# Attention outputs in three stages produced transposed, with a pair's values as stationary operand and both heads' weights as 256 moving columns

## The reference

```python
def _memory_attention(qm, mem, mem_norm, w_mem_kv):
    kv = _rmsnorm(mem, mem_norm) @ w_mem_kv
    s = jnp.einsum('bshd,bmhd->bhsm', qm, mk) * (HEAD_DIM ** -0.5)
    p = jax.nn.softmax(s, axis=-1)
    o = jnp.einsum('bhsm,bmhd->bshd', p, mv)
...
    # layer B, own block
    p = jax.nn.softmax(jnp.where(kpos <= qpos, s_own, NEG), axis=-1)
    o = jnp.einsum('bhqk,bkhd->bqhd', p_own, v_own)
    x = x + jnp.concatenate([o_self, o_mem], axis=-1) @ b_w_out[j]
...
    # layer C
    logits = jnp.where(valid[:, None], logits + bias, -jnp.inf)
    p = jax.nn.softmax(logits, axis=-1)
    out_a = jnp.einsum('bhtk,btkd->bthd', p, vg)
    x = x + jnp.concatenate([out_a, out_b], axis=-1) @ w_out[l]
```

## Time and profile before

| what | value |
|---|---|
| median of 3 runs | 915.58 us (914.89 to 916.04) |
| profiled execution, first to last instruction | 915.4 us |
| PE busy | 907.2 us, 99% of the span |
| PE weight loads | 767.8 us, 84% |
| DVE, ACT, POOL busy | 593.7, 490.4, 61.3 us |
| granted TensorE clock, mean of the span | 0.996 of full speed |
| chain that ended last | PE 96%, DVE 2%, ACT 1% |

### The profile page before, as it was taken

The page is one execution under the profiler, slowest core; times in us unless marked ns, Lnnn a source line. Parts: engine busy times, 40 slices in busy tenths (PEclk is TensorE's granted clock), DMA queues, the critical chain, the costliest instruction groups (busy, mean ns, idle before and its releaser), DMA issues.

```text
span 915.4 us, 13523 instructions
## 1 busy us (share of the span) xinstructions
PE 907.2 (99%) x4824; PEld 767.8 (84%) x4824; DVE 593.7 (65%) x898; ACT 490.4 (54%) x750; POOL 61.3 (7%) x124
## 2 busy tenths in 40 slices
PE   9999999999999999999999999999999999999998
PEld 7778788888888888888888888888788888888887
DVE  4768858555555686746855555667987466555565
ACT  6756666444444566754644444465577464444452
POOL 1102122000000000000200000013130000000000
PEclk9999999999999999999999999999998999999999
DMA  8945137665555453424966555545441447556551
GB/s 297 335 139 183 49 138 236 212 196 183 183 188 193 168 176 103 134 97 149 328 204 197 199 186 184 148 137 197 170 161 43 142 139 230 184 183 188 190 172 47
DMA packets 96885, 159.88 MB, mean 175 GB/s; under 512 B 5969, under 2 KB 37921, under 8 KB 96841
## 3 DMA queue, kind: packets, MB, share of 16 engines
q1 hardware_dynamic: 94240, 155.08, 51.1%
q10 hardware_dynamic: 2568, 4.21, 1.3%
q0 software_dynamic: 32, 0.02, 0.0%
HBM read 158.21 MB, written 3.16 MB: 176 GB/s over the span
## 4 chain that ended last, share of the span: by engine, by line
PE 96%; DVE 2%; ACT 1%; issue 0%; POOL 0%; ACTq 0%; POOLq 0%; DVEq 0%
PE turn L1660 10%; PE proj L1660 9%; PE proj L1604 6%; PE proj L1606 6%; PE proj L1605 6%; PE score L1604 6%; PE score L1605 6%; PE score L1606 6%; PE outp L1604 5%; PE outp L1606 5%; PE outp L1605 5%; PE turn L1664 5%; PE proj L1664 5%; PE outp L1839 3%; PE score L1802 2%; PE turn L1650 2%
## 5 line engine op out<-in xcount | busy, mean ns | idle before, releaser
L1931 DVE TENSOR_TENSOR wlo<-raw,whi 128x2048 fp32r<-128x2048 f32 (+1 forms) x131 | 297.3, 2278 | 171.8 <-ACT whi L1350 132.7
L1350 ACT ACTIVATE whi<-raw 128x2048 fp32r<-128x2048 f32 x64 | 122.7, 1917 | 162.5 <-PE turn L1664 76.2
L1339 ACT ACTIVATE whi<-raw 128x2048 fp32r<-128x2048 f32 (+1 forms) x67 | 126.3, 1896 | 63.3 <-PE proj L1606 16.9
L1604 PE MATMUL proj<-whi,set 128*128 128x512 f32 (+1 forms) x270 | 106.6, 395 | 0.0
L1606 PE MATMUL proj<-whi,set 128*128 128x512 f32 (+1 forms) x270 | 103.8, 384 | 0.0
L1605 PE MATMUL proj<-wlo,set 128*128 128x512 f32 (+1 forms) x270 | 103.5, 383 | 0.0
L1660 PE MATMUL turn<-set,whi 128*128 128x512 f32 x384 | 96.3, 393 | 0.0
L1660 PE MATMUL proj<-set,whi 128*128 128x512 f32 x384 | 95.6, 391 | 0.0
L1604 PE MATMUL score<-whi,set 128*128 128x512 f32 x236 | 93.0, 394 | 0.0
L1605 PE MATMUL score<-wlo,set 128*128 128x512 f32 x236 | 92.1, 390 | 0.0
L1606 PE MATMUL score<-whi,set 128*128 128x512 f32 x236 | 92.0, 390 | 0.0
(11 more groups left out here) (231 smaller groups left out, 1318.5 us busy)
## 6 DMA issues: line engine op xcount, KB each, us to landing
raw<-in_a_w_up SPq DMA_DIRECT2D x32, 512.0 KB, 4.3
raw<-in_a_w_down SPq DMA_DIRECT2D x32, 512.0 KB, 4.5
raw<-in_b_w_up SPq DMA_DIRECT2D x32, 512.0 KB, 4.4
raw<-in_b_w_down SPq DMA_DIRECT2D x32, 512.0 KB, 4.5
raw<-in_w_gate SPq DMA_DIRECT2D x22, 512.0 KB, 4.0
raw<-in_w_up SPq DMA_DIRECT2D x22, 512.0 KB, 5.0
raw<-in_w_down SPq DMA_DIRECT2D x22, 512.0 KB, 4.1
raw<-in_a_w_in SPq DMA_DIRECT2D x20, 512.0 KB, 6.7
```

What stands on the lines that cost most here:

```text
L1339: return act.activation(shaped(whi, u)[:, ks, :], shaped(raw, u)[:, ks, :], ACT.Copy)
L1350: act.activation(shaped(whi, u), shaped(raw, u), ACT.Copy).then_inc(hi_done, 1)
L1604: pe.matmul(out_, hi, wh, start=start, stop=False)
L1931: return dve.tensor_tensor(shaped(wlo, u)[:, ks, :], shaped(raw, u)[:, ks, :], shaped(whi, u)[:, ks, :], ALU.subtract)
```

## The change

For memory, causal and selected items (the differential ones stay as they are):

- `mix` multiplies `e` in place by the reciprocals, both heads in one DVE instruction of 2n columns, and `turn_weights` waits for it (`w_done`).
- `attend` takes the values of the pair, 128x128, as the standing operand and lets the transposed weights of both heads move, 256 columns, once per block of keys. The output is [values of two heads, head, query], and of its four quadrants of 64x128 two are wanted.
- The evacuation writes operands directly: ACT copies the two quadrants to the high part (`o_hi`), DVE subtracts for the low part (`o_evac`). For layer A's memory items these lie in a new buffer, `mem_out`; `operand()` finds them.
- `turn_operand` of outputs goes: half of the second bank pair in layer A, both in layer B, that of the selected heads in layer C. What a wait for it was is now a wait for `o_evac`.
- The key/value tile `qk` has 20 blocks instead of 24, one bias table and the late gains move to other buffers, and the value shared by selected heads is copied twice, side by side.
- The tables of `MOVES` for PE, DVE and ACT are new and longer, and POOL gets one.

```diff
--- before.py
+++ after.py
...
-        ("multiply 74", "turn_operand 34"), ("turn_weights 38", "attend 36"), ("turn_weights 37", "attend 35"),
...
+        ("turn_weights 39", "multiply 74"), ("turn_weights 38", "turn_weights 39"),
...
+    "POOL": [
+        ("split 6", "diff_norm 0"), ("multiply 6", "split 6"), ("statistics 1", "multiply 6"),
...
+        mem_out = sb("mem_out", [P, 2, 2, TOK], F32R)
...
-        def turn_operand(src, half, gains, ready, set_free, cols=None):
-
-            use = [t_use(), t_use()]
-            for b in range(2):
+        def operand(lhs, part, k):
+
+            if lhs == MEM_OUT:
+                return mem_out[:, k - 6, part, :] if k >= 6 else sets[1][:, k, part, :]
+            return sets[lhs][:, k, part, :]
+
+        def turn_operand(src, half, gains, ready, set_free, banks=2):
+
+            use = [t_use() for _ in range(banks)]
+            for b in range(banks):
                 st = add("turn_operand")
                 st.src, st.half, st.gains, st.ready, st.set_free = src, half, gains, ready, set_free
                 st.b, st.use, st.hi = b, use, count.hi
-            count.hi += 2
+            count.hi += banks
...
-        def attend(it, vneed):
+        def attend(it, vneed, lhs=1):
             it.o, it.o_free = o_use()
             it.vneed = vneed
             if it.kind == "diff":
                 count.osq += 1
                 it.osq = count.osq
+            else:
+                count.out += 1
+                k = it.pair + (6 if it.kind == "mem" else 0)
+                it.out, it.turned = count.out, [operand(lhs, part, k)[:, tok(it.t)] for part in range(2)]
             st = add("attend")
...
-        def finish_attention(w, items, o_half, last_qset_unit, oset, gain, vneed, around):
+        def finish_attention(w, items, o_half, last_qset_unit, gain, vneed, around):
 
             ua, ub, uc, ud = out_units(w)
-            o1 = turn_operand(o_nat, 0, [(None, oset, 0)], (o_evac, o_half), 2 * last_qset_unit + 2)[-1]
+            diff = items[0].kind == "diff"
+            o1, lhs = (o_evac, o_half), 1
+            if diff:
+                o1, lhs = turn_operand(o_nat, 0, [(None, 1, 0)], o1, 2 * last_qset_unit + 2)[-1], MEM_OUT
             attend(items[0], vneed); attend(items[1], vneed)
             turn_weights(items[2]); turn_weights(items[3])
-            if items[0].kind == "diff":
+            if diff:
                 norm(items[0:2])
 
             def last_items():
                 done = around()
                 attend(items[2], vneed)
                 o_all = attend(items[3], vneed)
-                if items[0].kind == "diff":
+                if diff:
                     norm(items[2:4])
                 return o_all, done
 
-            o_all, done = multiply_around(last_items, ua, oset, 0, o1, "P", True, False)
+            def last_turned():
+                if not diff:
+                    return o_evac, o_all
+                return turn_operand(o_nat, 1, [(None, 1, UK)], (o_evac, o_all), 0, banks=1)[-1]
+
+            o_all, done = multiply_around(last_items, ua, lhs, 0, o1, "P", True, False)
             split(ua + AHEAD)
-            o2 = multiply_around(lambda: turn_operand(o_nat, 1, [(None, oset, UK)], (o_evac, o_all), 0)[-1],
-                                 ub, oset, 0, o1, "S", True, False)
-            return out_tail(ub, (uc, oset, UK, o2), (ud, oset, UK, o2), 1 - oset, gain), done
+            o2 = multiply_around(last_turned, ub, lhs, 0, o1, "S", True, False)
+            return out_tail(ub, (uc, lhs, UK, o2), (ud, lhs, UK, o2), 0, gain), done
...
-        o1 = turn_operand(o_nat, 0, [(None, 1, 0)], (o_evac, o_a), 0)[-1]
+        o1 = (o_evac, o_a)
...
-                    elif it.kind == "idx":
+                    else:
                         act.wait_ge(o_full, it.o + 1)
-                        act.wait_ge(w_done, it.w)
                         for c in range(2):
-                            at = it.pair * P + c * DH
-                            ins = act.activation(o_nat[:, it.t, at:at + DH], Ob[it.o % 2][:, c * DH:(c + 1) * DH],
-                                                 ACT.Copy, scale=it.rs[:, c:c + 1])
-                        ins.then_inc(o_evac, 1)
+                            ins = act.activation(it.turned[0][HALF[c]], Ob[it.o % 2][HALF[c], tok(c)], ACT.Copy)
+                        ins.then_inc(o_hi, 1)
...
-                        ins = act.activation(v[:, t, 512:512 + DH], Sb[s % 2][:, t * P + DH:t * P + P], ACT.Copy)
+                        value = Sb[s % 2][:, t * P + DH:t * P + P].unsqueeze(1).broadcast_to([P, 2, DH])
+                        ins = act.activation(v[:, t, 512:512 + P].rearrange("p (c n) -> p c n", c=2), value, ACT.Copy)
...
-                    if it.kind == "diff":
-                        pe.wait_ge(w_done, it.w)
-                    else:
-                        pe.wait_ge(exp_done, it.exp + 1)
+                    pe.wait_ge(w_done, it.w)
...
-                    for c in range(1 if it.kind == "diff" else 2):
-                        for k in range(nk):
-                            b = c * nk + k
-                            wt = wT[:, it.buf, b * P:(b + 1) * P]
-                            h = 2 * it.pair + c
-                            dst = O[:, c * DH:(c + 1) * DH]
-                            if it.kind == "diff":
-                                val, dst = v[:, k, it.pair * P:(it.pair + 1) * P], O[:, 0:P]
-                            elif it.kind == "mem":
-                                val = memkv[:, 1, k * 256 + h * DH:k * 256 + (h + 1) * DH]
-                            elif it.kind == "causal":
-                                val = v[:, k, h * DH:(h + 1) * DH]
-                            else:
-                                val = v[:, k, 512:512 + DH]
-                            ins = pe.matmul(dst, wt, val, start=k == 0, stop=k == nk - 1)
+                    cols = slice(it.pair * P, (it.pair + 1) * P)
+                    for k in range(nk):
+                        if it.kind == "diff":
+                            wt = wT[:, it.buf, tok(k)]
+                            ins = pe.matmul(O[:, 0:P], wt, v[:, k, cols], start=k == 0, stop=k == nk - 1)
+                            continue
+                        if it.kind == "mem":
+                            val = memkv[:, 1, k * 256 + it.pair * P:k * 256 + (it.pair + 1) * P]
+                        elif it.kind == "causal":
+                            val = v[:, k, cols]
+                        else:
+                            val = v[:, k, 512:512 + P]
+                        wt = wT[:, it.buf, 0:2 * it.n].rearrange("p (c n) -> p c n", c=2)[:, :, tok(k)]
+                        ins = pe.matmul(O[:, 0:TOK].rearrange("p (c n) -> p c n", c=2), val, wt, start=k == 0,
+                                        stop=k == nk - 1)
                     ins.then_inc(o_full, 1)
...
                 elif st.kind == "mix":
                     it = st.it
                     dve.wait_ge(exp_done, it.exp + 1)
-                    ins = dve.reciprocal(it.rs, it.rs)
+                    behind(dve.reciprocal(it.rs, it.rs))
                     if it.kind == "diff":
-                        behind(ins)
                         behind(dve.tensor_tensor(it.rs[:, 1:2], it.rs[:, 1:2], lam[:, 4:5], ALU.mult))
                         e0, e1 = e[:, it.buf, 0:it.n], e[:, it.buf, it.n:2 * it.n]
                         behind(dve.tensor_scalar(e1, e1, it.rs[:, 1:2], None, ALU.mult))
                         ins = dve.scalar_tensor_tensor(out=e0, in0=e0, scalar=it.rs[:, 0:1], in1=e1,
                                                        op0=ALU.mult, op1=ALU.subtract)
+                    else:
+                        both = heads_view(e[:, it.buf, 0:2 * it.n], 2)
+                        ins = dve.tensor_tensor(both, both, spread(it.rs, it.n), ALU.mult)
                     ins.then_inc(w_done, 1)
                 elif st.kind == "attend":
                     it = st.it
-                    O = Ob[it.o % 2][:, 0:P]
-                    at = it.pair * P + (SELF if it.kind == "mem" else 0)
-                    dst = o_nat[:, it.t, at:at + P]
-                    if it.kind not in ("diff", "idx"):
-                        dve.wait_ge(o_full, it.o + 1)
-                        dve.wait_ge(w_done, it.w)
-                        dve.tensor_tensor(heads_view(dst, 2), heads_view(O, 2), spread(it.rs, DH), ALU.mult)\
-                           .then_inc(o_evac, 1)
+                    if it.kind != "diff":
+                        dve.wait_ge(o_hi, it.out)
+                        for c in range(2):
+                            ins = dve.tensor_tensor(it.turned[1][HALF[c]], Ob[it.o % 2][HALF[c], tok(c)],
+                                                    it.turned[0][HALF[c]], ALU.subtract)
+                        ins.then_inc(o_evac, 1)
...
```

(8 more changed lines are left out.)

28 lines of the change are left out of this document (16 added, 12 removed), and 183 rows, old and new, of the table MOVES.

## The result

| | before | after |
|---|---|---|
| median of the runs beside each other (5 each) | 915.58 us (914.89 to 917.16) | 921.83 us (920.85 to 922.03) |
| profiled execution, first to last instruction | 915.4 us | 919.4 us |
| that execution's own time | not listed | 921.14 us |

The change made the kernel slower: ratio 1.0061, 95% interval 1.0050 to 1.0072. I had forecast 914.9 and a range up to 918.6.

What follows compares the result with a forecast made beforehand. PE, busy 99% of the span, was taken as the bound, with its waits. Terms +0.7 - 3.05 - 0.6 - 0.2 + 1.6 + 0.9 = -0.65 us on the profiled 915.4, 0.2 under the median, gave 914.9; range 911.0 to 918.6.

Steps and rivals of the forecast that it cites:

- (a): Attend on PE's row: 92 instructions of 256 columns at 0.225 us replace 184 of 64 columns, +0.7 us (0 to +1.5).
- (b): Transposes of outputs on PE: 28 of 64 go and all of it counts, -3.05 us (-3.1 to -2.9).
- (c): Start: eight transposes of the memory input fill PE's wait for the first weights, -0.6 us, or 0.
- (d): Layer A's last output: the 0.9 us wait for the operand's DVE half comes behind two attends, -0.2 us (-0.9 to 0).
- (f): Start of stage C's selected heads: select rounds and multiplies stand ahead of steps PE needs, +0.9 us (0 to +1.5).
- the memory stages' waits, put at 0: Memory stages: weight products hide reciprocal and multiply (0.6 to 0.85 us), so 0; if the cover goes, +2 us.
- (e): End of the causal heads, where nothing covers: ACT's 10.1 us beside PE's 9.1 adds waiting, +1.6 us (-0.8 to +3).
- The recorded walk: End of the causal heads, stepped through from the end of the value products: 2.0 to 2.8 us late, 0.8 there before.
- stage C keeps its clock: Rival, stage C: its waits fall apart into short ones and 3.4 us of lost clock comes back, 911.5 us; chance 0.10.
- The waits are covered: Rival, causal heads' end and stage C's selected start: the added waiting there is 0, 912.4 us; chance 0.22.
- The causal stretch loses the clock: Rival, causal stretch: PE's pauses add up to 2 to 3 us and the clock falls, 918.3 us; chance 0.16.
- DVE sets the pace in the memory stages: Rival, memory stages: DVE gets 0.6 to 0.85 us more per item, +2 us, 916.9 us; chance 0.08.

Runs made afterwards that it cites:

- second profile: Kernel before, unchanged, timed and profiled again: 915.49 us median, the profiled execution with a span of 913.8 us.
- e10: Before, with 12 filling identity transposes in stage C's wait and the memory input's second half turned ahead of the first weight products: 914.76 us.
- e5: After, with the low part of one weight block moved behind the norm of items d8, d9 on DVE in layer A: 920.58 us.
- e2: After, without the multiply of e by the reciprocals; turn_weights of memory, causal and selected items waits for the exponentials alone: 918.17 us.
- e6: After, with ACT's copy of c5's turned weights moved ahead of the exponentials of c6 and c7: 922.96 us.
- e11: After, with ACT's output copies of 28 items doubled, the extra ones to a spare tile nobody reads: 929.32 us.
- e12: After, without the multiply of e, with layer A's low part behind the norm and stage C's wait filled with identity transposes: 915.47 us.
- e3: After, with three places of its order changed, on DVE (layer A, causal stretch, stage C) and ACT (copies of turned weights): 927.33 us.

## Why the prediction was wrong

**The miss.** The time is 6.9 us above the forecast. 1.5 of it is the last step of the sum, from the span to the time: I took 0.2 for it, and it is 1.7 (921.14 for a span of 919.4 after, 915.52 for 913.8 before). Another 0.7 is after's median above its profiled execution. The other 4.7 are the three attention parts, which against the first profile missed by 3.0 (A), 1.2 (B) and 0.5 us (C).

**What held.** (a) and (b), by after's groups:

```profile
L1922 PE MATMUL outp<-wT,v 128*128 128x256 f32 x60 | 16.0, 388 | 0.7 <-ACT wT L1574 0.5
...
L1922 PE MATMUL outp<-wT,memkv 128*128 128x256 f32 x32 | 8.1, 382 | 0.5 <-issue 0.5
...
L1737 PE MATMUL turn<-ident,o_nat 128*128 128x128 f32 x36 | 5.8, 304 | 0.2
```

92 instructions of 256 columns; two take 0.43 us from start to start at 392.84 below, 0.215 each against the 0.225 that I took, so 92 cost 19.8 us for 20.0 before: -0.2 where the term had +0.7. 36 transposes are left of 64. (c) The start saved: 0.4 to 0.7 as measured by e10, for 0.6. (d) The wait of 0.9 became 0.8, but the term had its place wrong: in before it stands at 114.78 and 115.38, ahead of transposes of e, and not at the last output, whose transposes at 125.04 waited for nothing. (f) Behind the gain op, DVE's timeline reads

```profile
687.84 1.66 DVE L2383 TENSOR_TENSOR o_nat<-o_nat,zq 128x512 f32<-128x512 f32 x1
689.53 0.43 DVE L2354 MAX8 stat<-wT 128x8 f32<-128x256 f32 x1
...
690.51 0.29 DVE L2239 CUSTOM_DVE_ANT_0 e<-score,memkv 128x128 f32<-128x128 f32 x1
```

with 2.67 us from the gain op to the maxima at 690.51. In before the gain op starts at 684.27 and the maxima at 685.96, 1.69 later. That is the round of 0.98 that the term names. Turn_weights starts 5.3 us behind the gain op (693.16) instead of 3.8 (688.11), for a forecast of 1.2 more.

**What failed first: the memory stages' waits, put at 0.** The step read "I put it at 0; if the cover goes, eight items would show up to 0.25 each". Attention A missed by 2.6 us. e5 accounts for 1.25 of it, a collision of DVE and GpSimd that no term had, and e2 for 0.8, the multiply. That 0.8 is the memory stage: in e2 the wait of 0.49 ahead of the memory attend at 92.69 is gone, and this attend starts at 92.03. So the cover went at one place, and the multiply's price was put at 0 for it. The other 0.5 is not isolated.

**Second, the size of (e).** The mechanism was right and the size was not. PE's timeline of after from attend c2 to attend c8:

```profile
392.84 0.59 PE L1922 MATMUL outp<-wT,v 128*128 128x256 f32 x2
...
399.04 0.63 PE L1899 MATMUL turn<-ident,e 128*128 128x128 f32 x4 [0.88 <-ACT wT L1574]
...
402.89 1.10 PE L1922 MATMUL outp<-wT,v 128*128 128x256 f32 x4 [0.49 <-ACT wT L1574]
...
405.04 0.70 PE L1922 MATMUL outp<-wT,v 128*128 128x256 f32 x2
405.54 0.51 PE L1691 MATMUL proj<-whi,set 128*128 128x512 f32 x1
```

12.7 us for 9.1 of work, 3.6 of waiting; before had 0.8. So the term was +2.8, forecast at +1.6 and bounded by +3. The chain there names who held PE:

```profile
397.14 0.68 ACT e L1583 x3
...
398.00 0.27 ACT set L1595
...
398.29 0.61 ACT wT L1574
...
399.04 0.64 PE turn L1899 x4
...
402.19 0.61 ACT wT L1574
...
402.89 1.12 PE outp L1922 x4
```

It is ACT's row of exponentials, output copies and weight copies, as worked out (10.1 us beside 9.1). The recorded walk has no wait for c5's weights. It puts ACT's exponentials of c6 and c7 at 2.2 to 3.9 us from the end of the value products, and they ran at 3.1 to 4.9, since DVE took the maxima of c6 only behind four subtractions:

```profile
394.17 1.21 DVE L2262 TENSOR_TENSOR set<-outp,set 64x128 fp32r<-64x128 f32 x4
395.41 0.29 DVE L2239 CUSTOM_DVE_ANT_0 e<-score,cmask 128x128 f32<-128x128 f32 x1
```

The copy of c5's weights stood behind them, at 398.29. e6 shows that taking it ahead does not help, e11 that more of the same costs half its length, and e12 that 2.2 of the 2.8 stay when the multiply is gone.

**Third, what stood at (f) besides the term.** Attention C missed by 2.5 against the second profile. e2 gives 1.5 of it to the multiply, where I had 0.3. The clock gives 0.5 net: PE's wait there grew to 2.18 us,

```profile
691.71 0.38 PE L1885 MATMUL score<-selmask,identb 128*128 128x128 bf16 x4 [2.18 <-DVE stat L2239]
```

and the low clock came behind it in each profile of the change with that wait left open. Here my reading of before was wrong at the base. I took the earlier trace rows for what before does and "stage C keeps its clock" for a rival in which the change gains 3.4. Before keeps its clock throughout in 24 of 70 executions, and of after's five none does, so the fall is a loss that comes and goes before and is nearly regular with the change (e2 has one execution of eleven at full clock, e11 one of four). The +0.2 between span and median hid this; the offset is 1.7.

**The rivals.** "The waits are covered" fell by e2, e5 and e11. "The causal stretch loses the clock" did not occur in after (its windows there read 1.00) but did in e3 once waits of 0.8 and 1.5 stood together. "DVE sets the pace in the memory stages" was nearest to attention A, by another mechanism. No single rival reached 921.8; the range had them one at a time, and what happened was more waiting in all three attention parts at once.

**The ledger,** on 915.4, before's time at full clock: about -3.7 on PE's row (-3.05 transposes, -0.2 attend from start to start, -0.4 the start), +3.7 multiply (3.0 by the spans), +1.25 collision, +1.0 clock with its waits (0.5 by the landmarks). That makes 917.7; the remainder to 921.8 is some 4.2 us, with an uncertainty of about 1 from the two measures. 2.2 of it is the waiting of the causal stretch that e12 still has, where PE waits for ACT's copies of weights. ACT's new output copies in that row are the likeliest owner by e11, the new orders themselves another; this split stays open, since no run has the new attend without copies.

## What to carry to other kernels

A saving on the bound engine has to be set against the links that it adds where nothing covers: here 28 transposes (3 us) were bought with a multiply, two copies and two subtractions for each of 28 items, on queues that were already the pace in the tight stretches. Count what each engine has to do between two points of PE's row and compare sums; where another engine's is the larger, that is the price, and moving a step within its row need not change it (e6). And take a second profile before reading a fall of the clock as a property of the kernel.

## What the hardware showed that I had not expected

- An op on 128x2 elements of GpSimd took 2.35 us beside a DVE subtraction of 128x2048 that began with it, and 0.19 us without (e5); it cost the kernel 1.25 us.
- The same program with the same wait of 1.5 us on PE ran on at full clock in one profile and at 0.66, 0.50, 0.50, 0.64 in another (spans 913.8 and 915.4); 24 of its 70 executions have a mean clock of 1.000. Twelve transposes of the identity in that wait kept eleven executions of eleven in the faster group.
- Full clock behind the wait gave back 1.7 us of 3.4 in before and 1.0 of 1.7 in after (0.5 by the landmarks): in before at half clock a later wait of 0.8 is gone.
